# A third weight unit beside the pair behind three norms, and position weights folded on VectorE

## The reference

```python
# first block, its end
h = h + g1 * mix
u = rmsnorm(h, norm2_w) * (1.0 + sc2) + sh2                    # norm 1
ff = (silu(u @ w_ffn_gate) * (u @ w_ffn_up)) @ w_ffn_down      # 1024 -> 2816 -> 1024
x = rmsnorm(h + g2 * ff, final_norm_w)                         # its own norm: "raw sums"
# second block
h = modulate(rmsnorm_2(x, norm_mix_g), sh1, sc1)               # norm 2
proj = h @ w_in                                                # q, k, v, gates, merge
kc = compress(k_cmp, cmp_pos_k, cmp_w1_k, cmp_w2_k); vc = compress(v_cmp, ...)
...                                                            # attention, merge, w_out
h = modulate(rmsnorm_2(x, norm_ffn_g), sh2, sc2)               # norm 3
x = x + g2 * swiglu(h, w_ffn_gate, w_ffn_up, w_ffn_down)
```

## Time and profile before

| | |
|---|---|
| time, median of 3 runs | 1474.66 us (1473.84, 1474.66, 1480.75) |
| time of the profiled execution | 1473.02 us |
| its span | 1471.2 us |
| mean granted TensorE clock | 0.991 |
| TensorE busy | 1445.6 us, 98% |
| VectorE busy | 937.3 us, 64% |
| ScalarE busy | 412.9 us, 28% |
| GpSimd busy | 94.9 us, 6% |

### The profile page before, as it was taken

How to read it: one execution, slowest core, us unless ns; L and a number is a source line. 1 busy time by engine, 2 the same in 40 slices (tenths; PEclk the granted TensorE clock), 3 DMA queues, 4 the chain that set the end, 5 groups by cost and what they waited for, 6 DMA issues and landing times.

```text
span 1471.2 us, 19416 instructions
## 1 busy us (share of the span) xinstructions
PE 1445.6 (98%) x7240; PEld 1174.3 (80%) x7240; DVE 937.3 (64%) x1666; ACT 412.9 (28%) x838; POOL 94.9 (6%) x75
## 2 busy tenths in 40 slices
PE   8999999999999999999999999999999999999997
PEld 7888777778888888888877777788887888888886
DVE  8887797886676665566566668765565444544443
ACT  6335355231111111013345456410122222221011
POOL 0100000200000001225100000000120000000110
PEclk9999999999999999999999999999999999999998
DMA  9444421436556564533221111123322232233332
GB/s 369 183 158 141 146 77 51 149 130 206 187 191 194 186 195 138 159 93 116 74 71 44 44 51 42 46 93 101 101 85 93 93 99 101 86 100 93 95 96 89
DMA packets 52464, 175.26 MB, mean 119 GB/s; under 512 B 5936, under 2 KB 6320, under 8 KB 52400
## 3 DMA queue, kind: packets, MB, share of 16 engines
q1 hardware_dynamic: 52400, 174.41, 36.0%
HBM read 172.29 MB, written 2.10 MB: 119 GB/s over the span
## 4 chain that ended last, share of the span: by engine, by line
PE 91%; DVE 4%; DMA 1%; ACT 1%; issue 1%; SPq 0%; ACTq 0%; DVEq 0%
PE bank L669 20%; PE bank L671 20%; PE bank L670 20%; PE bank L1182 8%; PE bank L1202 2%; PE bank L1237 2%; PE bank L1213 2%; PE bank L1036 2%; PE bank L861 2%; PE bank L863 2%; PE bank L862 2%; DMA fraw<-in_w_in_dram 1%; PE bank L895 1%; PE bank L834 1%; PE bank L835 1%
## 5 line engine op out<-in xcount | busy, mean ns | idle before, releaser
L669 PE MATMUL bank<-uh,wh 128*128 128x512 f32 x808 | 316.7, 392 | 6.1 <-DVE wl L1736 4.5
L670 PE MATMUL bank<-ul,wh 128*128 128x512 f32 x808 | 315.5, 390 | 0.0
L671 PE MATMUL bank<-uh,wl 128*128 128x512 f32 x808 | 315.5, 390 | 0.0
L1734 DVE CAST wh<-wraw 128x1024 fp32r<-128x1024 f32 (+1 forms) x223 | 147.8, 663 | 194.4 <-PE bank L671 178.8
L1736 DVE TENSOR_TENSOR wl<-wraw,wh 128x1024 fp32r<-128x1024 f32 (+1 forms) x223 | 261.4, 1172 | 7.7
L669 PEld LDWEIGHTS bank<-uh,wh 128*128 128x128 f32 x808 | 152.4, 189 | 38.9 <-issue 5.8
L671 PEld LDWEIGHTS bank<-uh,wl 128*128 128x128 f32 x808 | 152.4, 189 | 32.1
L670 PEld LDWEIGHTS bank<-ul,wh 128*128 128x128 f32 x808 | 152.5, 189 | 31.6
L669 PE MATMUL bank<-hh,wh 128*128 128x512 f32 x352 | 137.5, 391 | 0.0
L671 PE MATMUL bank<-hh,wl 128*128 128x512 f32 x352 | 137.0, 389 | 0.0
L670 PE MATMUL bank<-hl,wh 128*128 128x512 f32 x352 | 137.0, 389 | 0.0
(11 more groups left out here) (362 smaller groups left out, 2263.3 us busy)
## 6 DMA issues: line engine op xcount, KB each, us to landing
ada<-in_w_ada_dram SPq DMA_DIRECT2D x94, 512.0 KB, 4.7
wraw<-in_w_in_dram SPq DMA_DIRECT2D x61, 512.0 KB, 3.4
wraw<-in_w_ffn_gate_dram SPq DMA_DIRECT2D x44, 512.0 KB, 3.4
wraw<-in_w_ffn_up_dram SPq DMA_DIRECT2D x44, 512.0 KB, 3.4
wraw<-in_w_ffn_down_dram SPq DMA_DIRECT2D x32, 512.0 KB, 3.5
wraw<-in_w_ffn_down_dram SPq DMA_DIRECT2D x16, 384.0 KB, 3.1
wraw<-in_w_out_dram SPq DMA_DIRECT2D x16, 256.0 KB, 2.7
wraw<-in_w_out_dram SPq DMA_DIRECT2D x8, 512.0 KB, 3.4
```

What stands on the lines that cost most here:

```text
L669: nc.tensor.matmul(bank[:], a, rh[:, k0 + k, :], start=(first and k == 0), stop=False)
L670: nc.tensor.matmul(bank[:], a, rl[:, k0 + k, :], start=False, stop=False)
L671: mm = nc.tensor.matmul(bank[:], b, rh[:, k0 + k, :], start=False, stop=(last and k == nk - 1))
L1734: V.tensor_copy(wh[:, slot, 0:n], wraw[:, slot, 0:n]).then_inc(w_hi, 1)
```

## The change

Behind norms 1, 2 and 3 a third unit gets a place of its own outside the slots (`wxh`, `wxl`). VectorE casts it ahead of `norm_u`'s first tile (`third_hi`) and subtracts after `ul` of tile 1 (`third_lo`). TensorE's `passes_three` takes the place of `passes_both`; the third unit writes bank 2. Behind norm 2 the raw sums stand after tile 1 of the pair, and the two `qa2` units write banks 2 and 3. In `ff1` and `ff2` the first two iterations stand outside the loop on three engines; VectorE splits the fourth unit ahead of `hf` of iteration 0. GpSimd's folding of the position weights goes; VectorE does it in 32 instructions on 128x128, 18 ahead of the split of the fourth unit and 14 behind it.

```diff
@@ gpsimd
-            g.wait_ge(c_in, 64)
-            for n, pos in enumerate((POS_K, POS_V)):
-                ...
-                nc.gpsimd.tensor_tensor(wpos[:], w1c[:, n], vt2[:, pos:pos + 16].unsqueeze(2).broadcast_to([P, 16, P]),
-                                        ALU.mult).then_inc(c_pos, 1)
-                for level, k in enumerate((8, 4, 2, 1)):
...
@@ tensor
-            def passes_both(banks, slots, rh, rl, n_before):
+            def passes_three(ph, banks, n, n_before):
...
+                def third(k):
+                    if k == 0:
+                        pe.wait_ge(w_split, ph.u0 + 3)
+                    a, b = wxh[n][:, k * P:(k + 1) * P], wxl[n][:, k * P:(k + 1) * P]
+                    nc.tensor.matmul(B[2][:], a, uh[:, k, :], start=(k == 0), stop=False)
+                    nc.tensor.matmul(B[2][:], a, ul[:, k, :], start=False, stop=False)
+                    mm = nc.tensor.matmul(B[2][:], b, uh[:, k, :], start=False, stop=(k == KT - 1))
...
+                pair(0)
+                pair(1)
+                if n == 1:
+                    raw_sums()
+                third(0)
+                third(1)
+                for k in (2, 3):
+                    pair(k)
+                    third(k)
+                for k in range(4, KT):
+                    pair(k)
+                for k in range(4, KT):
+                    third(k)
...
-            simple("kc2", uh, ul, 2 * KT)
-            pe.wait_ge(ssr_ok, 7)
...
-            simple("qa2", uh, ul, part=(0, 1))
+            passes_three(PH["kc2"], (B[PH["kc2"].u0 % 2], B[(PH["kc2"].u0 + 1) % 2]), 1, 2 * KT)
+            passes(B[3], take(PH["qa2"], 0, 1), KT, uh, ul, 0, True, True)
@@ vector
+            def third_hi(u, n):
+
+                v.wait_ge(w_in[u % 2], 16 * (u // 2 + 1 - FRONT // 2))
+                V.tensor_copy(wxh[n][:], wraw[:, u % 2, :]).then_inc(w_hi, 1)
...
             def norm_u(nu, shift):
+                u = PH[("ff1", "kc2", "ff2")[nu - 1]].u0 + 2
+                third_hi(u, nu - 1)
...
+                    if t == 2:
+                        third_lo(u, nu - 1)
...
-                body(0, begun=True)
+                ahead(ph, 1, 0)
+                body(0, begun=2)
+                for j in MOD_AFTER.get(ph.u0 + 2, ()):
+                    modulation(j)
+                body(1, begun=1)
...
+            def fold_positions(js):
+                ...
+                            v.wait_ge(c_pos, 2 * j + n - 1)
+                            V.scalar_tensor_tensor(wfin[:, n], w1c[:, n, j], vt2[:, pos + j:pos + j + 1], wfin[:, n],
+                                                   op0=ALU.mult, op1=ALU.add).then_inc(c_pos, 1)
...
-            ahead(PH["kc2"], 0, 1)
+            v.wait_ge(c_in, 64)
+            fold_positions(range(9))
+            ahead(PH["qa2"], 0, 0)
+            fold_positions(range(9, 16))
             v.wait_ge(r_std, 1)
             V.reciprocal(rcolr, stdr).then_inc(r_col, 1)
-            ahead(PH["qa2"], 0, 0)
```

More of the change, by code:

```diff
@@ L672, in passes, with pair @@
                 mm.then_inc(unit_done, 1)
-            def passes_both(banks, slots, rh, rl, n_before):
-                for k in range(KT):
+            def passes_three(ph, banks, n, n_before):
+                slots = take(ph, 0, 0), take(ph, 0, 1)
+                def pair(k):
                     pe.wait_ge(n_uh, n_before + k + 1)
@@ L680, in passes_both @@
                         b = wl[:, slot, k * P:(k + 1) * P]
-                        nc.tensor.matmul(bank[:], a, rh[:, k, :], start=(k == 0), stop=False)
-                        nc.tensor.matmul(bank[:], b, rh[:, k, :], start=False, stop=False)
+                        nc.tensor.matmul(bank[:], a, uh[:, k, :], start=(k == 0), stop=False)
+                        nc.tensor.matmul(bank[:], b, uh[:, k, :], start=False, stop=False)
                     pe.wait_ge(n_ul, n_before + k + 1)
@@ L693, in take, with raw_sums, simple @@
                 return (ph.u0 + c) % 2
-            def simple(name, rh, rl, n_before=None, part=None):
+            def raw_sums():
+                pe.wait_ge(ssr_ok, 7)
+                for j in range(NT):
+                    mm = nc.tensor.matmul(B[6][:, j:j + 1], ssr[:, j * P:(j + 1) * P], ones[:, 0:1], start=(j == 0),
+                                          stop=(j == NT - 1), skip_group_check=True)
+                mm.then_inc(r_sum, 1)
+            def simple(name, rh, rl, part=None):
                 ph = PH[name]
                 def body(i):
-                    if n_before is not None and isinstance(i, int) and i == 0:
-                        slots = take(ph, 0, 0), take(ph, 0, 1)
-                        pe.wait_ge(drain_a, ph.a0)
-                        passes_both((B[ph.u0 % 2], B[(ph.u0 + 1) % 2]), slots, rh, rl, n_before)
-                    else:
-                        for c in range(2):
-                            slot = take(ph, i, c)
-                            pe.wait_ge(drain_a, i * 2 + (ph.a0 + c - 1))
-                            passes(B[(ph.u0 + c) % 2], slot, KT, rh, rl, 0, True, True)
-                over(pe, name, body, peel=n_before is not None, part=part)
+                    for c in range(2):
+                        slot = take(ph, i, c)
+                        pe.wait_ge(drain_a, i * 2 + (ph.a0 + c - 1))
+                        passes(B[(ph.u0 + c) % 2], slot, KT, rh, rl, 0, True, True)
+                over(pe, name, body, part=part)
             def out_proj(name, rh, rl, ready):
@@ L1092, in _ @@
             keep_busy(5, B[2])
-            ffn("ff1", KT, H1)
+            ffn("ff1", 0, KT, H1)
             down("down1", 0)
@@ L1098, in _ @@
             keep_busy(6, B[2])
[L1101 to L1107 removed]
+            pe.wait_ge(drain_a, PH["kc2"].a0)
+            passes_three(PH["kc2"], (B[PH["kc2"].u0 % 2], B[(PH["kc2"].u0 + 1) % 2]), 1, 2 * KT)
+            passes(B[3], take(PH["qa2"], 0, 1), KT, uh, ul, 0, True, True)
             spread(B[6], rcolr, r_col, 1, r_rstd)
@@ L1575, in _ @@
             A(stdr, B[6][:, 0:NT], ACT.Sqrt, bias=epst).then_inc(r_std, 1)
-            drain("qa2", qa, 0, ACT.Copy, part=(0, 1))
+            for c in range(2):
+                act.wait_ge(unit_done, PH["qa2"].u0 + c + 1 + U1)
+                A(qa[:, c, :], B[2 + c][:], ACT.Copy).then_inc(drain_a, 1)
             for n in range(2):
```

78 lines of the change are left out of this document (42 added, 36 removed).

## The result

The changed kernel took **1465.42 us** (median of 7 runs, 1464.19 to 1467.10), the kernel before 1473.84 in the runs beside it (7 runs, 1471.89 to 1480.75): a ratio of 0.9946 (95% interval 0.9934 to 0.9957), 8.4 us less. Measured again later, it took 1466.22 (6 runs) against 1471.89 (23 runs), a ratio of 0.9954 (0.9940 to 0.9969). Over all runs of the two kernels, those beside the experiments too, the medians are 1465.77 (13 runs) and 1472.69 (112 runs): 6.9 us less, by resampling 5.8 to 7.9. The forecast was a gain of 4.4 and a time of 1470.3 in a range of 1467 to 1476: too little gain, and a time 4.9 us too long.

A forecast was written before the change was run, and what follows sets the result against it. TensorE, busy 98%, was taken as the bound, so only its gaps and slow stretches could be won: 1.5 + 1.1 + 1.8 = 4.4 us off 1473.02 gives 1468.6, and with 1.64 for a median 1470.3, range 1467 to 1476.

The forecast's parts named there:

- The starting point: Whole kernel before: the profiled execution's 1473.02 us, with the median of the runs 1.64 above it.
- Norm 3, gain 1.5: Behind norm 3: the fifth unit starts at 22.7 us from the pair's first matmul, where it was 24.2.
- Norm 1, gain 1.1: Behind norm 1: the sixth unit starts after 29.34 us, before 30.4, because VectorE's modulations delay later splits.
- the two gaps: TensorE's idle 1.97 us before the third unit and 0.60 before the fourth in norm 1, costing 3.1 us.
- Norm 2, gain 1.8: Behind norm 2: first matmul of the pair to `spread` takes 24.2 us, where it took 26.0.
- 18.1 + 18p: Norm 2: when `spread` can start, in us from the pair's first matmul, with 18 folds of p each; 24.2 forecast.
- Rival (a): Norm 2: folds and GpSimd's tables block each other in full, losing 3.9 us, 1476.0 in all; 15 in 100.
- The slow clock's part in it: Norm 2: at most 3.3 us of the 26.0 can be won, including what TensorE's stretch at 1.2 GHz costs.
- rival (d): TensorE's clock falls behind raw sums inside norm 2's pair, costing 1.5 us, 1471.8 in all; 10 in 100.
- the fold's pace p: Norm 2: VectorE's time for each 128x128 fold, taken as 0.34 us, between 0.27 and 0.38 in full sequence.
- Rival (c): All three norms: new waits cost nothing and modulations are absorbed, winning all gaps, 8.6 us, 1466.1; 8 in 100.
- the new waits: TensorE, norms 1 and 3: 0.45 us on the third's subtraction, 0.25 on `hf`; norm 1 also 0.25 and 0.85.

The follow-up runs named there:

- n3_only: The kernel before with the third unit in the pair behind norm 3 alone: 1472.05 us, ratio 0.9995 to the kernel before.
- mods_later: The changed kernel with two of ff1's modulations moved from behind the fourth unit's split to behind later splits: 1466.52 us, ratio 0.9959 to the kernel before.
- raw_behind: The changed kernel with norm 2's raw sums put back behind the three units, ahead of the fourth: 1467.06 us, ratio 0.9952 to the kernel before.
- all_poolfold: The changed kernel with the position weights folded on GpSimd again: 1469.29 us, ratio 0.9980 to the kernel before.
- n1_only: The kernel before with the third unit in the pair behind norm 1 alone: 1470.35 us, ratio 0.9982 to the kernel before.
- before_busy: The kernel before with six small matmuls in the 1.57 us wait behind norm 2's raw sums: 1473.23 us, ratio 1.0002 to the kernel before.
- fill_13: The kernel before with seven small matmuls in the 2.0 us waits behind norms 1 and 3: 1472.01 us, ratio 0.9991 to the kernel before.
- lead_late: The changed kernel with VectorE's low part of ff1's first unit moved behind the last residual tile: 1466.93 us, ratio 0.9951 to the kernel before.

## Why the prediction was too small

The forecast was 4.5 us above the median of all runs of the changed kernel (1470.3 and 1465.77): 2.0 of these are the starting point, and 2.5 a gain that was priced too low.

**The starting point, 1474.66: too high by 2.0.** The prediction took the median of three runs, 1.64 above the profiled execution. Over 112 runs the kernel before has 1472.69, 0.3 below that execution. With 4.4 us less than this the forecast would have been 1468.3.

**Norm 3, gain 1.5: right.** Measured 1.43 in the profiles (35.03 to 33.60), the fourth unit at 17.15 for 17.19. `n3_only` shows it alone.

**Norm 1, gain 1.1: right.** 35.89 to 34.78, the sixth unit at 29.19 for 29.34, its wait 0.69 for the predicted 0.85. The forecast that most of what the two gaps give is lost again two units later held; `mods_later` adds that the modulations were not alone, a transfer stood behind them.

**Norm 2, gain 1.8: the mis-sized term.** The sum "18.1 + 18p" was right in form and p was wrong: 0.34 was taken, 0.283 measured (0.255 without the tables). 18 x 0.057 = 1.0 us is the whole difference between 24.2 and 23.2. At 0.283 the fourth unit's wait is next to nothing, so a still quicker fold would win hardly more. Rival (a) fell: GpSimd's tables ran beside the folds and cost VectorE 0.03 us a fold, not their own length. The eight took 5.95 us, and 4.97 in `raw_behind`, where they ran mostly after the folds; the whole difference lies in two of them, 0.84 and 1.18 us long, that met VectorE's cast and subtraction of 128x1024, while five beside folds kept the 0.53 of one alone. The Trainium skill's rule ("SBUF — State Buffer", Terms), that the loser of the port pair is fully blocked, is not borne out for these small operations; it is for the wide ones, where the split took 4.6 us and not 2.0 (`all_poolfold`). A small loss was missed: the third's cast took 1.24 us beside GpSimd's addition and put the pair off by 0.26.

**"The slow clock's part in it": the reading of before was wrong, its total right.** The 26.0 us were taken as wait and slow clock. `n1_only` and `before_busy` show that the clock cost nothing there: behind it stood a split not yet ready, as slow as GpSimd's folding made it. The third unit removes the one wait (1.57), but the other goes only if the split is both away from GpSimd's folding and early enough, so neither half pays alone.

**The clock as a risk only: a term put at nothing.** The prediction counted the clock once, as rival (d), a loss. Waits of 2 us in norms 1 and 3 were priced at their own length. In 4 of 14 profiled cases seven or eight matmuls at 1.2 GHz stood behind such a wait, in none of 20 without one. They put the fifth unit off by 1.6 us in norm 3 and 0.7 in norm 1: on average 0.5 and 0.2 us, 0.7 for both. With 1.1, 1.4 and norm 2's 2.8 - 0.3 that makes 5.7, just below what all runs give (6.9, 5.8 to 7.9). That the half clock comes of the wait is not shown beyond these counts; `fill_13`'s time agrees in size (0.8 us) but its interval holds nothing too. Left open: why `n1_only`'s runs have as high a mean clock (0.9931) as nearly the whole change, and `n3_only`'s (0.9905) none of it, and with it some 1.2 us that no stretch shows.

**So the steps that failed** are two terms of the sum, the fold's pace p (0.34 for a measured 0.283, 1.0 us) and the clock behind the waits (nothing for some 0.7), and the time it was taken from (2.0); some 1.2 us of the gain stay without a cause. Rival (c)'s time, 1466.1, is close to the measured one, but not by its mechanism: the new waits came much as forecast.

**The rest is chance.** The first comparison gave 8.4 where all runs give 6.9, and the profiled pair shows 3.0 us in two stretches where TensorE's work is the same. Of the profiles with norm 1's way in short (2.5 us to the spread), two are of kernels with the old norm 1 and two with the new; the others have 3.6 to 4.5, but for `lead_late`. What was won in norm 2 was kept up to norm 3: the scores apart, the stretches between agree within 0.1 us in both kernels.

## What to carry to other kernels

Before pricing a slow or idle stretch, ask what the engine would have met had it come earlier: here a half clock was free because a split behind it was late, and two edits paid only together. Take the starting time from as many runs as the forecast is meant to be compared with; the median of three was 2 us off, nearly half the gain forecast. A wait on TensorE costs its length and sometimes slow matmuls around it, so price its removal with both, and take the difference of two profiled executions stretch by stretch: what differs where the code does not is chance, and a second profile of the same kernel shows how much (5.2 us here). For instructions on VectorE and GpSimd side by side, the small ones here hardly held each other up and the wide ones did; the nearest row of the same size is the better guide.

## What the runs showed that was not expected

- 128x128 folds on VectorE follow each other by 0.255 us on average, 0.283 beside GpSimd's 128x128 table instructions, though the trace gives some 340 to 350 ns for one.
- The cast and the subtraction of 128x1024 took 0.71 and 1.23 us alone, 2.35 and 2.18 beside GpSimd's additions of 128x1024 and less (`all_poolfold`).
- Of a VectorE subtraction (128x1024) and a GpSimd addition (128x512) that meet, one is stretched: VectorE's to 2.26 us for 1.23 where GpSimd began 0.11 us earlier, GpSimd's to 2.35 for 1.28 where both began together. 1.5 us of the path hang on it.
- Behind a wait of 4.27 us TensorE lost 2.8 us to 13 matmuls and more at 1.2 GHz, behind waits of 2.0 us 1.6 us in eight matmuls (6 of 16 cases), or nothing.
